# The end of a two-block transformer kernel on one core: token tile 0 finished first, the last 64 outer-product tokens laid out in halves over 128 partitions, gathered tokens normed beside the outer units

## What is computed

```python
def layer_norm(x, g, b):
    mu = jnp.mean(xf, axis=-1, keepdims=True)
    var = jnp.mean(jnp.square(xf - mu), axis=-1, keepdims=True)
    y = (xf - mu) * lax.rsqrt(var + LN_EPS)
    return (y * g + b)

# peer_ffn: expert and gate are found per token and head
        u_sel = u[expert]
        v_sel = v[expert]
        act = jax.nn.gelu(jnp.einsum('td,thkd->thk', xc, u_sel), approximate=False)
        return jnp.einsum('thk,thkd->td', (gate * act), v_sel)

    h = layer_norm(ALPHA * h + mix, ln1_g[l], ln1_b[l])
    ffn = peer_ffn(h, peer_wq[l], peer_subkeys[l], peer_u[l], peer_v[l])
    h = layer_norm(ALPHA * h + ffn, ln2_g[l], ln2_b[l])
```

## Time and profile before

| | us |
|---|---|
| median of 3 runs | 2902.71 |
| lowest and highest run | 2898.66, 2905.43 |
| span of the profiled execution, first to last instruction | 2895.8 |
| TensorE busy in that span | 2784.9 (96%) |
| DVE, ACT, POOL busy | 1940.6, 1363.5, 388.4 |
| mean granted TensorE clock | 0.990 |

### The profile page before, as it was taken

One profiled execution on the slowest core, in us unless ns is written; L12 is line 12 of the kernel. 1 busy time (PEld: TensorE's weight loads), 2 busy tenths in 40 slices (PEclk: granted clock), 3 DMA queues, 4 the chain that ended last, 5 costly groups with the idle time before them and its releaser, 6 DMA issues.

```text
span 2895.8 us, 46048 instructions
## 1 busy us (share of the span) xinstructions
PE 2784.9 (96%) x19224; PEld 2627.5 (91%) x19224; DVE 1940.6 (67%) x2900; ACT 1363.5 (47%) x2223; POOL 388.4 (13%) x360
## 2 busy tenths in 40 slices
PE   7999999999999999999989999999999999999996
PEld 6999989888999998999989999998888999988785
DVE  7556578554435545564658657767887888878886
ACT  5356454455545334444453124434555555555554
POOL 0000010211110000005000002221222111113320
PEclk9999999999999999999999999999999999999998
DMA  5444455433325554544534569998999988899894
GB/s 225 172 155 153 159 158 193 135 109 101 100 97 185 180 177 162 188 146 162 180 118 161 186 233 360 365 356 332 368 374 374 341 326 322 319 356 366 339 355 145
DMA packets 109678, 668.44 MB, mean 231 GB/s; under 512 B 25776, under 2 KB 26312, under 8 KB 31552
## 3 DMA queue, kind: packets, MB, share of 16 engines
q1 hardware_dynamic: 83808, 496.08, 46.8%
q0 software_dynamic: 24512, 164.97, 15.6%
q10 hardware_dynamic: 1152, 4.47, 0.4%
HBM read 651.54 MB, written 13.30 MB: 230 GB/s over the span
## 4 chain that ended last, share of the span: by engine, by line
PE 71%; DVE 13%; DMA 9%; ACT 5%; issue 2%; SPq 0%; POOL 0%; DVEq 0%; ACTq 0%
PE PS L1093 71%; DVE WL L1723 5%; DMA raw<-in_pv 4%; DVE m L1714 4%; DMA m<-in_pv,keep 3%; ACT WH L2497 2%; ACT m L2478 1%; DVE m L1967 1%; PE PS L1096 1%; DMA m<-s_kk 1%; ACT m L2479 1%; DVE m L1964 0%; DMA raw<-in_w_kv 0%; DVE m L2318 0%; ACT L2478 0%
## 5 line engine op out<-in xcount | busy, mean ns | idle before, releaser
L1723 DVE TENSOR_TENSOR WL<-raw,WH 128x1024 fp32r<-128x1024 f32 x804 | 988.1, 1237 | 591.2 <-ACT WH L2497 589.2
L2497 ACT CAST WH<-raw 128x1024 fp32r<-128x1024 f32 x804 | 836.9, 1046 | 529.2 <-PE PS L1093 357.3
L1093 PE MATMUL PS<-m_4096r,WH 128*128 128x256 f32 x5184 | 976.9, 289 | 24.5 <-DVE WL L1723 12.9
L1093 PEld LDWEIGHTS PS<-m_4096r,WH 128*128 128x128 f32 x5184 | 812.8, 193 | 44.4 <-issue 24.9
L1093 PE MATMUL PS<-m_4096r,WL 128*128 128x256 f32 x2592 | 736.2, 284 | 0.0
L1093 PE MATMUL PS<-m_8192r,WH 128*128 128x256 f32 (+1 forms) x2560 | 559.8, 313 | 8.8 <-issue 5.4
L1093 PE MATMUL PS<-WH,m_896r 128*128 128x512 f32 x1536 | 521.8, 392 | 12.7 <-DVE m_896r L2411 9.1
L1093 PEld LDWEIGHTS PS<-m_4096r,WL 128*128 128x128 f32 x2592 | 499.2, 193 | 0.0
L1093 PEld LDWEIGHTS PS<-m_8192r,WH 128*128 128x128 f32 x2560 | 398.3, 194 | 10.7 <-issue 6.0
L1093 PE MATMUL PS<-m_8192r,WL 128*128 128x192 f32 (+1 forms) x1792 | 404.6, 272 | 0.0
L1093 PE MATMUL PS<-WL,m_896r 128*128 128x512 f32 x1024 | 400.3, 391 | 0.0
(11 more groups left out here) (246 smaller groups left out, 1807.6 us busy)
## 6 DMA issues: line engine op xcount, KB each, us to landing
raw<-in_pu SPq DMA_DIRECT2D x128, 1024.0 KB
raw<-in_pv SPq DMA_DIRECT2D x128, 1024.0 KB
raw<-in_w_qkv SPq DMA_DIRECT2D x48, 1024.0 KB
raw<-in_w_o SPq DMA_DIRECT2D x48, 1024.0 KB
raw<-in_w SPq DMA_DIRECT2D x40, 1024.0 KB
raw<-in_w_z SPq DMA_DIRECT2D x32, 1024.0 KB
raw<-in_w_kv SPq DMA_DIRECT2D x16, 1024.0 KB
raw<-in_w_q SPq DMA_DIRECT2D x16, 1024.0 KB
```

Of the source, the lines that this page charges most:

```text
L1093: return e.matmul(o, l, x, start=start, stop=stop)
L1723: tt(WL[:, k, :], raw[:, n % NRAW, h * 1024:h * 1024 + 1024], WH[:, k, :].bitcast(F), ALU.subtract).then_inc(S["lo"], 1)
L2497: e.copy(WH[:, k, :], raw[:, n % NRAW, h * 1024:h * 1024 + 1024]).then_inc(S["hi"], 1)
```

## The change

**Outer units.** Units 62 and 63 of the second half do all tile 0 matmuls first (`vm_first`), then the second tile's (`vm_last`). The number of matmuls in them is the same.

**Gathered tokens.** After `sp_sum`, whose last instruction now also sums, tokens 192 to 255 get their mean, `sp_root` (ACT: squares, square root), four `sp_norm` instructions of 64x1024 (DVE) and a store from the SP queue, one step per half unit. The fold of 64 rows of these tokens is as before.

**The other 64 tokens** (128 to 191) lie as 128 partitions x 1024: columns 0 to 1023 in the low partitions, 1024 to 2047 in the high ones (`BACC`). The residual comes in that shape (`HNB`), ACT copies the saved sums across (`residual(1)`), gain and bias are loaded once more in that shape (`ln_load`, four loads of 256 KB by the POOL queue before outer unit 40), and `end` folds by two ACT copies and DVE adds.

**`end`** norms tile 0 with sums that DVE takes along with the adds, while TensorE is still on the second tile's matmuls. TensorE's four folding matmuls of 512 columns become two of 2 columns.

```diff
@@ def sparse(self, st):
         self.do("sp_shift")
         yield
         self.do("sp_sum")
+        st["fast"] = True
+        yield
+        self.do("sp_root")
+        yield
+        for c in range(4):
+            self.do("sp_norm", c)
+            yield
+        self.do("sp_store")
@@ def peer(self, half, st):
+            if half and j == 40:
+                self.do("ln_load")
...
-                self.do("vm", half, j, n, h)
+                if half and j >= 62:
+                    self.do("vm_first", j, n, h)
+                else:
+                    self.do("vm", half, j, n, h)
...
             drain(st["sparse"])
+            for h in range(2):
+                for j in (62, 63):
+                    self.do("vm_last", j, PEER + 192 + j, h)
@@ sync_program
+            def sp_store():
+                s.wait_ge(*at("sp_out", 2))
+                e.dma_start(out[0, 192:256, :], XS[HIGH, :]).then_inc(S["st_sync"], 16)
@@ vector_program
-                v.step(stt(x, HN[LAST, 2048:4096], ALPHA, x, ALU.mult, ALU.add))
+                v.step(summed(x, HN[LAST, 2048:4096], ALPHA, x, stat(24)[LAST, :]))
+                v.own()
+                one(stat(25)[LAST, :], stat(24)[LAST, :], -1.0 / 2048, ALU.mult).then_inc(S["sp_mean"], 1)
+
+            def sp_norm(c):
+                o = slice(1024 * (c // 2), 1024 * (c // 2) + 1024)
+                x = XS[LAST, o]
+                if c == 0:
+                    v.wait_ge(*at("sp_root", 1))
+                    v.step(recip(stat(28)[LAST, :], stat(27)[LAST, :]))
...
+                if c % 2 == 0:
+                    v.step(stt(x, x, stat(25)[LAST, :], LG[LAST, o], ALU.add, ALU.mult))
+                else:
+                    stt(x, x, stat(28)[LAST, :], LB[LAST, o], ALU.mult, ALU.add).then_inc(S["sp_out"], 1)
@@ def residual(c):
+                elif c == 2:
+                    v.wait_ge(*at("b_shift", 2))
+                    v.step(stt(BACC, HNB, ALPHA, BT, ALU.mult, ALU.add))
+                else:
+                    v.own()
+                    tt(BACC[LOW, :], BACC[LOW, :], quarter(ACC, 2)[LOW, :], ALU.add).then_inc(S["b_sum"], 1)
+                    tt(BACC[HIGH, :], BACC[HIGH, :], quarter(ACC, 3)[HIGH, :], ALU.add).then_inc(S["b_sum"], 1)
@@ scalar program
+            def sp_root():
+                rows = slice(128 - NS, 128)
+                a.wait_ge(*at("sp_mean", 1))
+                a.step(act(GB[1][rows, :], XS[rows, :], ACT.Square, bias=stat(25)[rows, :], acc=stat(26)[rows, :]))
+                a.own()
+                act(stat(27)[rows, :], stat(26)[rows, :], ACT.Sqrt, scale=1.0 / 2048,
+                    bias=C("eps5")[rows, :]).then_inc(S["sp_root"], 1)
+
+            def residual(c):
...
+                e.copy(BT[LOW, :], quarter(ACC, 2)[HIGH, :]).then_inc(S["b_shift"], 1)
+                e.copy(BT[HIGH, :], quarter(ACC, 3)[LOW, :]).then_inc(S["b_shift"], 1)
@@ gpsimd_program
+            def ln_load():
+                g_.wait_ge(*at("b_shift", 2))
+                g_.wait_ge(*at("b_sum", 2))
+                for c, rows in enumerate((LOW, HIGH)):
+                    o = slice(1024 * c, 1024 * c + 1024)
+                    e.dma_start(LGB[rows, :], D["ln2g"][rows, o]).then_inc(S["ld_lnb"], 16)
+                    e.dma_start(LBB[rows, :], D["ln2b"][rows, o]).then_inc(S["ld_lnb"], 16)
```

More of the change, by code:

```diff
@@ L1705, in tensor_program @@
                   "h_turn": h_turn, "qs_out": qs_out, "s_turn": s_turn, "s_gate": s_gate, "g_mm": g_mm, "u_out": u_out, "c_begin": c_begin, "vm": vm,
-                  "end": end}).run()
+                  "vm_first": vm_first, "vm_last": vm_last, "end": end}).run()
         def vector_program(e):
@@ L1717, in one, with summed @@
                 return ts(o, a, s, None, op)
+            def summed(o, a, s, b, total):
+                return e.scalar_tensor_tensor(out=o, in0=a, scalar=s, in1=b, op0=ALU.mult, op1=ALU.add, accum_out=total)
             def lo_part(q):
@@ L2433, in end @@
-                v.wait_ge(*at("used", done(NUNIT - 1)))
-                for t in range(2):
-                    for d in range(4):
-                        x = OUT[t][:, d * 512:d * 512 + 512]
-                        if t == 0:
-                            tt(x, x, PS[:, d, :], ALU.add).then_inc(S["y2"], 1)
-                        else:
-                            v.wait_ge(*at("folded", d + 1))
-                            copy(x[0:64, :], PS[0:64, 4 + d, :]).then_inc(S["y2"], 1)
-                    v.wait_ge(*at("y2_sum", 4 * t + 4))
-                    v.step(e.tensor_reduce(stat(8 + t), stat(4 * t, 4), AX.X, ALU.add))
-                    v.own()
-                    one(stat(10 + t), stat(8 + t), -1.0 / 2048, ALU.mult).then_inc(S["y2_mean"], 1)
@@ L2446, in end @@
[L2446 to L2457 removed]
+                    x = OUT[:, d * 512:d * 512 + 512]
@@ new lines, in end @@
+                b = v.step(tt(b2(BACC[HIGH, :]), banks(6, HIGH), b2(BACC[HIGH, :]), ALU.add))
+                v.own(r)
+                stt(OUT[:, 0:1024], UA[:, 0:1024], stat(12), LB[:, 0:1024], ALU.mult, ALU.add).then_inc(S["out_a"], 1)
+                v.wait_ge(*at("b_low", 1))
+                v.wait_ge(*at("b_high", 1))
+                v.own(b)
+                v.step(summed(BACC, BT, 1.0, BACC, stat(15)))
+                v.own()
+                one(stat(16), stat(15), -1.0 / 1024, ALU.mult).then_inc(S["b_mean"], 1)
@@ new lines, in end @@
+                stt(OUT[:, 1024:2048], UA[:, 1024:2048], stat(12), LB[:, 1024:2048], ALU.mult,
+                    ALU.add).then_inc(S["out_a_more"], 1)
+                v.wait_ge(*at("b_fold", 1))
+                v.wait_ge(*at("b_mean", 1))
+                m = v.step(one(stat(18), PS[:, 0, 0:1], 0.5, ALU.mult))
+                v.own(m)
+                v.step(tt(stat(19), stat(16), stat(18), ALU.subtract))
+                v.own()
+                v.step(tt(stat(19), stat(19), stat(19), ALU.mult))
```

206 lines of the change are left out of this document (138 added, 68 removed).

## The result

The change takes **2914.49 us** (median of 10 runs, 2905.48 to 2920.62); the kernel before, run beside it, 2903.62 (10 runs). The ratio is **1.0038, 95% interval 1.0027 to 1.005**: about 11 us slower. The forecast was 2898.0, range 2892.5 to 2904.5, with 0.09 for slower by over 0.2%. It was wrong.

The account below looks back on a forecast made before the run. TensorE and the DMA engines (97% busy, 376 GB/s) were taken as near their limits together, with TensorE alone the chain from 2810.42. Terms -11.7 + 5.0 + 2.0 = -4.7 took 2902.71 to 2898.0 us, range 2892.5 to 2904.5.

Parts of the forecast that it names:

- The tail, - 11.7: After the last matmul: early norming of tile 0 shortens the stretch to the end from 25.9 to 14.2 us.
- The accumulator's read: In the tail, DVE's adds also writing a sum: between nothing and 0.19 us, a third of it counted on the path.
- the early tile does not help: Rival, tail: DVE's work behind the last matmul eats tile 0's head start; 3 us later gives 2901.0; chance 0.07.
- Unit 58, + 5.0: Units 58 to 60: gathered tokens' norm delays TensorE's inputs, 3.3 us at unit 58, growing to 5.0; bounds 3.3 and 6.8.
- the clock's fall: TensorE's clock after the stall at unit 58: about 1.5 us if it falls, mostly covered by unit 59's wait; taken as 0.
- the cover holds: Rival: norm work and the extra megabyte fall into idle time, TensorE loses 3 us in all; 2894.0; chance 0.23.
- `ln_load` and the rest, + 2.0: Extra 1 MB at outer unit 40: 2.8 us of all engines at 376 GB/s, taken as +2.0; bounds 0 and 4.3.
- the extra load collides with a gather once: Rival: a late gather holds DVE and `c_lo`, TensorE stands, its clock falls; price 4.3, result 2900.3; chance 0.17.
- `HN` in four pieces, 0: Loading `HN` in four pieces has the same bytes as before, so no cost was counted.
- The sum: Whole kernel: -11.7 + 5.0 + 2.0 = -4.7 us.
- My slower rival: Rival: gathers behind `ln_load` collide twice, 11.5 us in place of 2.0, clock's fall uncovered; 2909.0; chance 0.08.
- The forecast case: Whole kernel: the main outcome, around 2898.0 us, running from -8 to +1 by its bounds; chance 0.45.

Follow-up runs that it names:

- before again: The kernel before, executed once more with no edit, as a control: 2905.94 us, 1.0002 of the kernel before.

## Why the prediction was wrong

**The tail, - 11.7: right in kind and nearly in size.** From 25.9 to 15.3 is - 10.6, inside the bounds. The last instruction ends at E + 11.1 (worked out: E + 11.0). The missing 1.1 is the store: from there to the end are 4.2 us, and I had taken 3.05 from the earlier trace rows. The last two stores are of 256 KB and 64 partitions each; they land 3.0 and 3.7 us after their issue, where before's stores of 512 KB and 128 partitions land after 2.6. In this window of the change only one of them moves, and nothing else:

```profile
2909.00:2910.00 1.00, 0.00 (x0) 0.00 (x0) 0.00 (x0) 0.00 (x0) 0.00 (x0) 0.50 0.98 197
```

That is the low rate of `ln_load` again, in a store and beside nothing. I had priced the store by its bytes too. The accumulator's read, which I had guessed at a third of 0.19, is 0.08. Of the rival "the early tile does not help" nothing was seen.

**Unit 58, + 5.0: right, a little small.** The wait is 3.21 (forecast 3.3), released by `c_lo`, with the table load ahead of the casts. The casts came as worked out: the root ran 0.01 after its table load, so the drain of 1.38 us that the Trainium skill's page "ScalarE: Activation LUTs", section "What ACT_TABLE_LOAD costs", adds to each switch of tables is not seen here. From unit 57 to E the profile of the change lost 6.1 us against before (5.4 against before again). Behind the wait the mechanism was another than forecast: I had DVE hold TensorE 1.5 more ahead of unit 59 and the clock's fall covered by that. There is no wait ahead of unit 59; the clock fell (0.61 and 0.54, 11 matmuls in 4 us), so that unit 58's 20 matmuls took 6.4 us, and only 0.59 of waiting came, ahead of unit 60. That the size is near is in part luck. I had also looked for the clock's fall between idle times of 2.3 and 4.25, though before's own trace has one at S, 0.51 in the 2 us after an idle time of 2.75. The rival "the cover holds" is out by the profiles; in the runs, spreading the norm, which takes most of this wait away, gave back about 2 us in one pair of kernels and about 5 in the other.

**`ln_load` and the rest, + 2.0: the step that failed.** The sentence was "at 376 GB/s that is 2.8 us of all engines", with an upper bound of 4.3. The four loads alone, put into the kernel before, cost 8.7 us (5.5 to 11.9). Two things were wrong in it. I took the rate of the stretch as the rate of these loads. They fill 64 partitions each, and beside them the engines move 229 to 292 GB/s at the same busy share; as two plain loads of 128 partitions the same bytes move at 372 to 405 and cost 2.6 us (- 1.7 to 7.0), near the 2.0 of my sum, though the two intervals overlap. In the profiles the difference is clear: units 45 to 47 take 21.6 to 22.7 us in all four with the four loads, and 13.7 with the two, though in the change itself two plain loads leave them at 19.3. The Trainium skill spoke against it, and I had not weighed it: the page "DMA: Bandwidth & Descriptors", section "Rules for kernel authors", says of transfers to disjoint halves of the partitions to use one of 128 instead. And I added the price as if it could only be paid once, in bytes. It is paid by the instruction that waits: a late gather holds DVE, DVE's order holds `c_lo`, TensorE stands 5.5 us, and its clock falls. My rival "the extra load collides with a gather once" had exactly this chain, with a price of 4.3 and a chance of 0.17; in the profiles it cost 7 to 9. The stall at S + 230 with its fall of the clock is in all four profiles with these four loads at unit 40, and in none of the nine in which no part of this 1 MB is loaded there. Its chance should have been the main one.

**`HN` in four pieces, 0: wrong.** "The same bytes as before" is the same mistake. By itself it is + 3.8 (0.6 to 7.3) in the runs, and it shows as a stall of 3.7 to 10.1 near S + 34 in all eight profiles in which `LG` and `LB` follow the pieces.

**The sum.** - 10.6 + 6.1 + 8.7 + 3.8 = + 8.0, against + 10.9 measured (7.8 to 14.5); the intervals of the two load terms cover the rest. My slower rival, the collision twice over at 11.5, came to 2909.0 by another split: one collision was dearer than I made it, and the second was of the pieces I had counted as free. The forecast case was said to run from - 8 to + 1 by its bounds; the bounds of its three terms add up to - 9.6 and + 1.7, and the result lies far outside these too.

**The base.** The 2895.8 of the profiled execution was short by the time before S, not by anything in the stage; carrying the distance to the median was the right guard.

**What stays open.** Why loads of 64 partitions run at this rate I have not tested, nor whether the size of 256 KB or the number of loads has a part in it; the runs show only that these transfers do, beside other loads and alone. Whether plain loads cure the change cannot be said from one profile with a 3.6 us stall and intervals that overlap. Why a stall ahead of unit 30 comes in some executions is open too. `HN`'s pieces as plain loads of 128 partitions were not tried, as they would need another layout of the stored copy.

## What to carry to other kernels

Price an added DMA by its own shape, not by the stretch's GB/s: how many partitions it fills, and what its outermost dimension is. In a stretch where the DMA engines are full, ask whose data lies behind it in the same queue, and which engine waits for that in order; that wait is the price, and the bytes are only its start. Loads that are needed late should be started late, if the last stretch has the engines free: here that, together with the norm spread out and with no byte saved, turned a change that lost 7 to 11 us into one that gains 8 to 11.
